# Four small pads between the operand buffers of a one-core decoder kernel

## The reference, cut to what matters

```python
def swiglu(h, w_gate, w_up, w_down):
    return (jax.nn.silu(h @ w_gate) * (h @ w_up)) @ w_down

def moe_swiglu(h, router_w, router_b, w_gate, w_up, w_down):
    ...
    for e in range(N_EXPERTS):
        out = out + gates[..., e:e + 1] * swiglu(h, w_gate[e], w_up[e], w_down[e])
```

## Time and profile before

| | |
|---|---|
| runs, us | 1983.98, 1989.90, 1990.19 (median 1989.9) |
| profiled execution, first to last instruction | 1982.6 us |
| granted clock of the matrix engine, mean | 0.993 of full speed |
| busy: PE, weight loads, VectorE, ScalarE | 1932.9, 1716.3, 1460.4, 1221.9 us |
| chain that ended last, by engine | PE 83%, VectorE 5%, ScalarE 2% |
| DMA | 463.84 MB, mean 234 GB/s |

### The profile page before, as it was taken

One profiled execution on the slowest core, in us unless ns is written; L12 is line 12 of the kernel. 1 busy time (PEld: TensorE's weight loads), 2 busy tenths in 40 slices (PEclk: granted clock), 3 DMA queues, 4 the chain that ended last, 5 costly groups with the idle time before them and its releaser, 6 DMA issues.

```text
span 1982.6 us, 32400 instructions
## 1 busy us (share of the span) xinstructions
PE 1932.9 (97%) x12947; PEld 1716.3 (87%) x12947; DVE 1460.4 (74%) x1648; ACT 1221.9 (62%) x1464; POOL 59.3 (3%) x92
## 2 busy tenths in 40 slices
PE   8999999999999999999999999999999999999998
PEld 8888998999787888888888888899999998988997
DVE  6977777664888888888898988887565556746554
ACT  6774443655777777777777777647364445865443
POOL 2001000000000000000000000200000000000000
PEclk9999999999999999999999999999999999999999
DMA  7426555532889999999999999643045654334562
GB/s 239 132 86 213 192 191 180 160 128 107 329 322 395 347 395 357 395 357 395 358 395 359 394 359 390 239 143 108 2 145 181 201 175 144 112 122 145 184 199 85
DMA packets 267895, 463.84 MB, mean 234 GB/s; under 512 B 11297, under 2 KB 147854, under 8 KB 267790
## 3 DMA queue, kind: packets, MB, share of 16 engines
q1 hardware_dynamic: 264252, 450.47, 64.4%
q0 software_dynamic: 3152, 11.54, 1.5%
q10 hardware_dynamic: 386, 0.32, 0.0%
HBM read 453.92 MB, written 8.39 MB: 233 GB/s over the span
## 4 chain that ended last, share of the span: by engine, by line
PE 83%; DVE 5%; ACT 2%; issue 1%; DMA 0%; DVEq 0%; ACTq 0%; SPq 0%
PE bank L2769 23%; PE bank L2771 23%; PE bank L2770 23%; PE bank L2966 3%; PE bank L2968 2%; DVE w_lo L2272 1%; PE bank L3232 1%; DVE w_lo L1820 1%; ACT w_hi L1090 1%; PE bank L3065 1%; PE bank L3400 0%; PE bank L2878 0%; PE bank L3084 0%; PE bank L3422 0%; PE bank L3180 0%
## 5 line engine op out<-in xcount | busy, mean ns | idle before, releaser
L1820 DVE TENSOR_TENSOR w_lo<-ring,w_hi 128x2048 fp32r<-128x2048 f32 (+1 forms) x157 | 354.1, 2263 | 177.5 <-ACT w_hi L1090 177.1
L2272 DVE TENSOR_TENSOR w_lo<-ring,w_hi 128x2048 fp32r<-128x2048 f32 x144 | 329.5, 2291 | 57.0 <-ACT w_hi L1429 57.0
L2769 PE MATMUL bank<-w_hi,a_both 128*128 128x512 f32 (+1 forms) x976 | 359.2, 368 | 8.4 <-DVE w_lo L2272 4.8
L2771 PE MATMUL bank<-w_hi,a_both 128*128 128x512 f32 (+1 forms) x976 | 352.6, 361 | 0.0
L2770 PE MATMUL bank<-w_lo,a_both 128*128 128x512 f32 (+1 forms) x976 | 351.8, 360 | 0.0
L2769 PE MATMUL bank<-a_both,w_hi 128*128 128x256 f32 x1200 | 346.1, 288 | 5.4 <-DVE work L1937 2.1
L1090 ACT ACTIVATE w_hi<-ring 128x2048 fp32r<-128x2048 f32 x156 | 296.7, 1907 | 83.9 <-PE bank L2771 78.3
L2770 PE MATMUL bank<-a_both,w_hi 128*128 128x256 f32 x1200 | 340.6, 284 | 0.0
L2771 PE MATMUL bank<-a_both,w_lo 128*128 128x256 f32 x1200 | 340.5, 284 | 0.0
L1429 ACT ACTIVATE w_hi<-ring 128x2048 fp32r<-128x2048 f32 x144 | 276.1, 1918 | 100.5 <-PE bank L2771 67.0
L2272 DVE TENSOR_TENSOR w_lo<-work,w_hi 128x2048 fp32r<-128x2048 f32 x120 | 274.6, 2288 | 28.4 <-ACT w_hi L1429 28.4
(11 more groups left out here) (510 smaller groups left out, 2646.3 us busy)
## 6 DMA issues: line engine op xcount, KB each, us to landing
ring<-in_moe_w_up SPq DMA_DIRECT2D x72, 1024.0 KB, 10.7
work<-in_moe_w_gate SPq DMA_DIRECT2D x64, 1024.0 KB
ring<-in_moe_w_down SPq DMA_DIRECT2D x56, 1024.0 KB, 11.0
work<-in_moe_w_down SPq DMA_DIRECT2D x32, 1024.0 KB, 10.6
ring<-in_w_up SPq DMA_DIRECT2D x32, 1024.0 KB, 5.4
ring<-in_w_down SPq DMA_DIRECT2D x32, 1024.0 KB, 4.9
ring<-in_moe_w_gate SPq DMA_DIRECT2D x16, 1024.0 KB, 5.0
ring<-in_w_in_a SPq DMA_DIRECT2D x13, 1024.0 KB, 5.3
```

The source lines that it names most:

```text
L1820: V.tensor_tensor(lo, raw, hi.bitcast(F32), ALU.subtract).then_inc(lo_made, 1)
L2272: V.tensor_tensor(w_lo[:, slot, :], raw_tile(j), w_hi[:, slot, :].bitcast(F32), ALU.subtract).then_inc(m_lo, 1)
L2769: PE.matmul(out, left[0], right[0], start=start, stop=False, **kw)
L2771: return PE.matmul(out, left[1], right[0], start=False, stop=stop, **kw)
```

## The change

Four buffers that nothing reads or writes are allocated between the split buffers. They take 32, 160, 64 and 64 bytes of each partition. Everything allocated behind a pad moves up by it; no instruction, semaphore, queue or shape changes.

```diff
         ring = sb("ring", [P, SLOTS, TILE])
         w_hi = sb("w_hi", [P, SLOTS, TILE], F32R)
+        sb("apart_lo", [P, 8])
         w_lo = sb("w_lo", [P, SLOTS, TILE], F32R)
+        sb("apart_in", [P, 40])
         a_both = sb("a_both", [P, 2, DC, T], F32R)
         a_hi, a_lo = a_both[:, 0, :, :], a_both[:, 1, :, :]
+        sb("apart_act", [P, 16])
         act_hi = sb("act_hi", [P, 2, 2 * T], F32R)
+        sb("apart_act_lo", [P, 16])
         act_lo = sb("act_lo", [P, 2, 2 * T], F32R)
         x = sb("x", [P, DC, T])
```

## The result

The changed kernel takes 1993.9 us (median of 13 runs, 1989.4 to 1997.4) against 1988.0 (13 runs of the kernel before, 1980.3 to 1992.2): ratio 1.0035, 95% interval 1.0024 to 1.0047. It is slower by 0.35%, where 1958 us and a gain were forecast. The profiled execution has 1989.3 us against 1982.6, 6.7 more.

What follows compares the result with a forecast made beforehand. Taken to be bound by the pace of its split matmuls, the kernel was to gain 29.7 us on 256-column matmuls and 2.3 on wide pairs, 32 in all: 1989.9 - 32 = 1958 us, range 1930 to 1991.

Steps and rivals of the forecast that it cites:

- What bounds the kernel: Whole kernel: bound by the pace of its split matmuls, three lines holding 69% of the span, some 1368 us.
- The loss at 2.4 GHz is no work of the array, and an address sets the scatter apart: 256-column matmuls: 13.3 ns lost each at full clock; the scatter's 113.6 against 120.0 ns comes from its operands' unequal places.
- Hold each other up when both run through the same places modulo 512: All split matmuls: a weight load and the stream beside it hinder each other at equal places; the pads end this.
- For the others I take 113.6: 256-column matmuls at distances no row shows: the scatter's pace too; with all 5088 a gain of 32.6 us, 29.7 on the path.
- exactly the scatter's 192: The 3600 matmuls of project and pair_product: w_hi stationary and a_both moving get the scatter's distance of 192 bytes.
- 512 columns. I take nothing: 3936 matmuls with 512 columns: steady pace stays at 226.7 ns, their weight loads of 188 ns being the unhindered median.
- the sign that I had named for "right": 256-column matmuls: their weight loads were to fall from a median of 192 to 188 ns.
- Wide pairs: 352 pairs of a wide and a 256-column matmul, 353.3 ns each: half of a possible 4.6 us gained, 2.3 us.
- VectorE, ScalarE, DMA, and the cover: Other engines and transfers: no change from moved operands; with 5% less matmul time none of them becomes the bound.
- the slower one: Rival, chance 0.08: the 512-column streams hold their slower pace behind a stall, 5.0 ns more each, costing 19.7 us.
- In part: only the distance of 192 helps: Rival, chance 0.05: only that distance, or half of the streams, gains; 16 us, giving 1974 us.
- The rule of two read ports: Skill text against the forecast: loading weights takes nothing from the running matmul, so addresses can't matter and time stays 1990.

Runs made afterwards that it cites:

- e1: Streams alone, computing nothing of the reference: 48 matmuls at each distance from 0 to 480 bytes in steps of 32; 512 columns took 226.7 ns at 256, 233.1 at 192.
- e6: The streams of e1 again, at distances 0 to 240 bytes in steps of 16, upwards and back; at 112, 256 columns took 113.3 ns both ways.
- e7: Kernel before, with a_both 192 bytes and act_hi and act_lo 256 bytes behind the weights, no pad ahead of w_lo; 1972.3 us, ratio 0.9934.
- e10: The split's three matmuls as streams alone, at equal or mixed distances taken from the kernels, forwards and backwards; 256 columns all at 192 took 113.3 ns forwards.
- e4: Changed kernel without the 32-byte pad ahead of w_lo, the other buffers kept 192, 256 and 320 bytes behind the weights; 1972.3 us, ratio 0.9930 to the kernel before.
- e2: Kernel before with one pad only, 192 bytes ahead of a_both, moving all allocated behind it too; 1971.3 us, ratio 0.9933.
- e8: e7 with the experts' token columns in a_both beginning 16 columns, 64 bytes, further on; 1970.3 us, ratio 0.9924 to the kernel before.

## Why the prediction was wrong, by its own steps

*What bounds the kernel:* right. The product's lines hold the same share of the chain, and the time followed their pace.

*The loss at 2.4 GHz is no work of the array, and an address sets the scatter apart:* right in part. The distance alone moves 256 columns between 113.3 and 120.1 ns and 512 between 226.7 and 236.7 (e1, e6). The scatter, moved from 192 to 64, went from 113.6 to 117.9. But no distance brought the pace under 113.3 and 226.7, so of the 13.3 ns that the prediction called lost some 6.6 stay with 256 columns and all of them with 512, and what they are no run shows.

*"Hold each other up when both run through the same places modulo 512":* half right. It is modulo 256 (e1, e7), and the equal place is bad for 256 columns only, where 80 and 96 bytes are as bad (119.9 and 120.0 in e6). For 512 it is the best there is.

*"For the others I take 113.6":* this step failed first, with 5.4 us in place of 32.6. The scatter's row was one distance, 192, and in one of its two paces; I gave its pace to every unequal distance. The other places have 116.6 to 120.1, but for 112, and 64 in one of its two paces. Even the 3600 matmuls that I called "exactly the scatter's 192" were 192 in two steps out of three, the third being 160 for `w_lo`'s pad, and in that mixture the pace is 118.7 in the kernel (118.8 and 117.8 in e10). Without that pad the step is nearly right for these 3600: 115.1 in e4, 114.6 in e2, 18.8 of 23 us.

*"512 columns. I take nothing":* this step failed too, by 17.5 us. I had read 226.7 as a stream with the usual hindrance, and "unequal is better" as a rule for both widths. The weight load at 188 ns, which I took for the sign of an unhindered stream, tells nothing: it is 188 in the changed kernel too, at 231 ns a step. Nor is it done in the first half of the stream by its row, which covers 188 of 226.7 ns. With 256 columns the sign that I had named for "right" even came, a median of 188 instead of 192, at 118.7 ns a step:
```profile
L2773 PEld LDWEIGHTS bank<-a_both,w_hi x1200: 186/188/335, 15.1 to 1969.2; 128*128 128x128 f32 x172
```
In e1 the load's median is 192 for 256 columns at 0 and 256 alone; everywhere else it is 187 or 188, at any pace.

*Wide pairs:* 2.3 us forecast, 0.1 measured (353.4 to 353.0 a pair).

*VectorE, ScalarE, DMA, and the cover:* right. Their busy times are unchanged, and no new wait stands ahead of the matmuls; what came instead is that the experts' stalls gave back 4 us of the loss.

*The rivals:* the slower one had the place and almost the price, 19.7 us against 17.5, but I gave it 0.08, for two reasons that fell. I counted on the pace going back to 226.7 by itself, which the streams by themselves do at distance 0, and at 240 in one of two passes (e6). And I let it decide only from 8.1 ns a step, against a gain of 32 that wasn't there; against the 5.5 us that the rest of the matmuls gained it decides from 5.5 / 3936 = 1.4 ns, and 4.4 came. "In part: only the distance of 192 helps" was near the truth for the columns of 256, and said nothing of the 512.

*The rule of two read ports* (the Trainium skill, "TensorE: Matmul & The Clock Gate", "Step-by-step: what each phase is for"), from which I drew that the addresses couldn't matter: they do, with 226.7 against 233.1 ns in e1 for streams that differ in one buffer's place alone. Whether it is the weight load that takes from the stream, which is what that rule denies, no run shows, since no stream without weight loads was measured.

## What to carry to other kernels

One row of a stream at an odd address shows that addresses matter, not which address is good: before a layout is chosen, the streams are measured by themselves at every distance, for each width that the kernel has, and with the mixture of operands that the kernel gives them. What helps one width can be paid for by another (here 256 columns want 112 or 192 and 512 want 0), so operands with different needs get their own place, and the two halves of a split (`w_hi` and `w_lo`) stay at the same one. After the change the paces are read by kind of stream, since a mean over them hides a gain and a loss of the same size.

## What the runs showed of the hardware that I had not expected

- The pace of fp32r matmuls with a weight load each depends on the distance of moving and stationary operand modulo 256 bytes, down to steps of 16, and on its sign: 113.3 to 120.1 ns for 256 columns, 226.7 to 236.7 for 512 (e1, e6). At 1.2 GHz it doesn't show with 256 columns: the earlier trace rows have 213 ns at 0, and the changed kernel (1296.48 - 1294.35) / 10 = 213.0 at 192, 192, 160, in a stretch with a granted clock of 0.50:
```profile
1293.90:1297.10 3.20, 3.20 (x15) 3.18 (x16) 3.16 (x5) 3.18 (x4) 0.00 (x0) 0.50 1.08 365
...
1294.35 0.41 PE L2774 MATMUL bank<-a_both,w_hi 128*128 128x256 f32 x1
...
1296.48 0.41 PE L2775 MATMUL bank<-a_both,w_lo 128*128 128x256 f32 x1
```
- A stream at one and the same distance can hold different paces over the 48 steps that were run: 113.3 or 117.8 at 64 and 192, 117.2 to 120.0 at 160, 226.7 or 236.7 with 512 columns at 240, 228.9 or 233.3 with 512 columns at 64. The passes differ in what ran ahead. At 112 both passes came to 113.3, and so did the kernel's long stretches nearly (113.5 to 114.5 with their first steps).
- One step in three at another distance takes the whole stream off its pace: with 512 columns from 226.7 to 233.3 and 231.7 at 0, 32, 0 (e10), and in the kernel with 256 columns from mostly 113.7 to 118.7 at 192, 192, 160 (e4 against the changed kernel).
- Why it is so, the runs don't show. That it is the meeting of the stream with the weight load beside it fits that either operand's move does it (the moving one in e1, the stationary one in e8's 16 columns), but streams without weight loads were not measured.
